# Splitting the attention stage's first operands ahead of it, and laying five key blocks as three and two

## The reference, cut to what matters

```
s = einsum('...qgrd,...kgd->...qgrk', q, k) * SCALE
mask = (dpos >= 0) & (dpos < WINDOW)          # window branch; selected branch: dpos >= 0
p = softmax(where(mask, s, NEG))
o = gates[0] * o_cmp + gates[1] * o_sel + gates[2] * o_win
x = x + rmsnorm(concat(ret_y, o) @ w_o); ...  # then the MLP
```

## Time and profile before

| What | us |
|---|---|
| Median of 3 runs | 1829.54 (1827.85 to 1830.1) |
| The profiled execution's own time | 1826.82 |
| Its span, first to last instruction | 1825.2 |
| TensorE busy | 1713.0 (94%) |
| VectorE busy | 838.9 (46%) |
| ScalarE busy | 618.1 (34%) |
| Mean granted clock of TensorE | 0.978 |

### The profile page before, as it was taken

How to read it: one execution, slowest core, us unless ns; L and a number is a source line. 1 busy time by engine, 2 the same in 40 slices (tenths; PEclk the granted TensorE clock), 3 DMA queues, 4 the chain that set the end, 5 groups by cost and what they waited for, 6 DMA issues and landing times. The chain is left out here.

```text
span 1825.2 us, 29596 instructions
## 1 busy us (share of the span) xinstructions
PE 1713.0 (94%) x11664; PEld 1511.1 (83%) x11664; DVE 838.9 (46%) x1606; ACT 618.1 (34%) x1188; POOL 148.9 (8%) x261
## 2 busy tenths in 40 slices
PE   5999999995999779999989999999999999999997
PEld 4989988994864655555549889999999999999997
DVE  5556342131116366677775675322332233223476
ACT  5222322210010156666655554202320232023343
POOL 1000000013534300000000110000000000000011
PEclk9999999997999799999999999999999999999999
DMA  8111011144966500000017533211111111111365
GB/s 292 47 48 48 24 48 42 47 104 116 239 180 190 153 17 1 1 1 1 1 45 198 174 119 93 66 47 47 47 47 47 47 47 47 47 47 47 110 177 166
DMA packets 215500, 148.98 MB, mean 82 GB/s; under 512 B 13565, under 2 KB 204882, under 8 KB 214978
## 3 DMA queue, kind: packets, MB, share of 16 engines
q1 hardware_dynamic: 180050, 99.38, 19.4%
q0 software_dynamic: 12848, 37.47, 6.7%
q10 hardware_dynamic: 22464, 10.23, 2.2%
HBM read 134.76 MB, written 16.47 MB: 83 GB/s over the span
## 5 line engine op out<-in xcount | busy, mean ns | idle before, releaser
L2077 PE MATMUL psum<-act_hi,whi 128*128 128x344 f32 x960 | 310.2, 323 | 8.6 <-DVE wlo L2196 5.6
L2077 PE MATMUL psum<-act_lo,whi 128*128 128x344 f32 x960 | 307.4, 320 | 0.0
L2077 PE MATMUL psum<-act_hi,wlo 128*128 128x344 f32 x960 | 307.4, 320 | 0.0
L2196 DVE TENSOR_TENSOR wlo<-wraw,whi 128x1024 fp32r<-128x1024 f32 x111 | 136.0, 1225 | 253.7 <-ACT whi L2093 253.5
L2077 PE MATMUL psum<-hidden_hi,whi 128*128 128x344 f32 x768 | 246.4, 321 | 0.0
L2077 PE MATMUL psum<-hidden_hi,wlo 128*128 128x344 f32 x768 | 245.3, 319 | 0.0
L2077 PE MATMUL psum<-hidden_lo,whi 128*128 128x344 f32 x768 | 245.2, 319 | 0.0
L2093 ACT ACTIVATE whi<-wraw 128x1024 fp32r<-128x1024 f32 x111 | 117.4, 1057 | 338.1 <-PE psum L2077 332.0
L231 PE MATMUL psum<-act_hi,whi 128*128 128x344 f32 x648 | 214.8, 331 | 4.1 <-DVE act_lo L404 4.1
L231 PE MATMUL psum<-act_hi,wlo 128*128 128x344 f32 x648 | 208.1, 321 | 0.0
L231 PE MATMUL psum<-act_lo,whi 128*128 128x344 f32 x648 | 208.1, 321 | 0.0
(11 more groups left out here) (366 smaller groups left out, 2474.7 us busy)
## 6 DMA issues: line engine op xcount, KB each, us to landing
wraw<-in_w_down SPq DMA_DIRECT2D x48, 512.0 KB, 3.7
wraw<-in_w_up SPq DMA_DIRECT2D x40, 512.0 KB, 4.1
wraw<-in_w_in SPq DMA_DIRECT2D x27, 512.0 KB, 3.8
wraw<-in_w_o SPq DMA_DIRECT2D x23, 512.0 KB, 4.6
h_features<-mixed_then_h POOLq DMA_DIRECT2D x24, 172.0 KB, 2.5
h_again<-h_features POOLq DMA_DIRECT2D x24, 172.0 KB, 3.0
x_rows<-in_x_prompt SPq DMA_DIRECT2D x4, 1024.0 KB, 9.2
dec_pages<-in_cache_sel_k SPq DMA_DIRECT2D x64, 64.0 KB, 3.0
```

The costliest lines, as they stand in the source:

```text
L2077: last = pe.matmul(ps[:, u % 3, 0:TN], wt[:, kt, :], xt[:, kt, cols], start=(kt == 0 and i == 0), stop=(kt == KT - 1 and i == 2))
L2196: dve.tensor_tensor(m.wlo[p % 2][:], wraw[raw_slot[p]][:], m.whi[p % 2][:].bitcast(F32), ALU.subtract).then_inc(lo_ready, 1)
```

## The change

Four things are changed.

1. The bf16 cast of the compressed bias and the split of query block 7 move from the start of the attention stage into the cache stage: ScalarE's part stands after its last copy of turned probabilities and ahead of its issues of value pages, VectorE's cast ahead of the fold matrix, and VectorE's part of the split after the second request. TensorE no longer waits for them at the start of the attention stage.
2. The first tile of `w_o` is split in the attention stage, by ScalarE at step 20 and by VectorE at step 21, into buffers of its own (`w_o_first_hi`, and `w_o_first_lo` over the raw tile). The raw tile lies elsewhere. The tail no longer splits it.
3. The first piece of attention outputs that the tail splits is cut in two, each with one row of tiles, and TensorE's unit 0 starts after the first of them.
4. Where five key blocks meet a query block they lie as three (384 columns, in the last three quarters of a bank) and two (256 columns, in the first half of the next). For the window the two are the oldest and the newest, read as one strided operand, and both masks are added by one bf16 matmul of 256 columns; the values are taken in the same order. The selected branch does it for query block 4, the window branch for blocks 4 to 7.

```diff
+            def three_and_two(bank, g, order, hi, lo, q):
+                a, b, c = order[0], order[3], order[4]
+                for n, k in enumerate((hi, lo)):
+                    pe.matmul(ps[:, bank, P:4 * P], q, k[:, g, a * P:(a + 3) * P], start=(n == 0), stop=(n == 1))
+                for n, k in enumerate((hi, lo)):
+                    pe.matmul(ps[:, bank + 1, 0:2 * P].rearrange("p (a n) -> p a n", n=P), q,
+                              k[:, g, 0:SEQ].rearrange("p (a n) -> p a n", n=P)[:, b:c + 1:c - b, :], start=(n == 0), stop=(n == 1))
...
-                if g == 0 and r == 0:
-                    pe.wait_ge(q_lo, 2 * ORDER.index(i) + 2)
+                if g == 0 and r == 0 and k:
+                    pe.wait_ge(q_lo, 2 * ORDER.index(i))
...
-                for a in range(lo, hi, 4):
-                    last = keys(2 + (a - lo) // 4, g, a * P, min(hi - a, 4) * P, win_hi, win_lo, q)
...
+                if i >= KW - 1:
+                    three_and_two(2, g, window_order(i), win_hi, win_lo, q)
+                    last = pe.matmul(ps[:, 3, 0:2 * P], m.ident_bf[:], m.edges_bf[:], start=False, stop=True, skip_group_check=True)
+                else:
+                    keys(2, g, 0, (i + 1) * P, win_hi, win_lo, q)
...
-            pe.wait_ge(casts, 1)
...
-            split_q(0)
             for k in range(len(steps) + 2):
...
+                if k == 20:
+                    act.wait_ge(first_loaded, 16)
+                    act.activation(m.first_hi[:], m.w_first[:], ACT.Copy).then_inc(first_hi, 1)
...
-            dve.tensor_copy(bias_bf[:], m.c("cmpbias").rearrange("p (a n) -> p a n", n=CP)).then_inc(casts, 1)
-            split_q(0)
...
+                if k == 21:
+                    dve.wait_ge(first_hi, 1)
+                    dve.tensor_tensor(m.first_lo[:], m.w_first[:], m.first_hi[:].bitcast(F32), ALU.subtract).then_inc(first_lo, 1)
...
+        def mix_parts(n):
+            a = n % 4
+            return (slice(0, 1), slice(1, 2)) if n == 0 else (slice(2 * a, 2 * a + 2),)
...
             split(0)
-            round_hi(0)
...
             split(0)
-            reduce_lo(0)
```

More of the change, by code:

```diff
@@ L1325, in _ @@
             act.activation(pnT[:], ps[0:DEC, 3, 0:2 * ROWS].rearrange("p (a b) -> p a b", b=ROWS), ACT.Copy).then_inc(p_copied, 1)
+            for e in range(2):
+                rows = slice(e * HD, (e + 1) * HD)
+                act.activation(m.q_split[(NB - 1) % 2][rows, :, e, :], m.nqT[rows, :, (NB - 1) * P:SEQ], ACT.Copy).then_inc(next_hi, 1)
             for b in range(4, DEC):
@@ L1477, in _ @@
             for b in range(DEC):
+                if b == 2:
+                    for e in range(2):
+                        rows, far = slice(e * HD, (e + 1) * HD), slice((1 - e) * HD, (2 - e) * HD)
+                        dve.wait_ge(next_hi, e + 1)
+                        dve.tensor_tensor(m.q_split[(NB - 1) % 2][far, :, e, :], m.nqT[rows, :, (NB - 1) * P:SEQ],
+                                          m.q_split[(NB - 1) % 2][rows, :, e, :].bitcast(F32), ALU.subtract).then_inc(next_lo, 1)
                 dve.wait_ge(v_used, b + 1)
@@ L1511, in stage_attend @@
         blk = [m.place(f"att_block_columns{i}", [P, 4, R], F32, m.ring + 22528 + 64 * i) for i in range(2)]
-        bias_bf = m.place("att_cmp_bias", [P, NB, CP], BF16, m.ring + 21888)
-        q_split = [m.place(f"att_q_split{i}", [P, NH // 2, 2, P], F32R, m.A + 57344 + 4096 * i) for i in range(2)]
+        q_split, bias_bf = m.q_split, m.bias_bf
         half = m.place("att_out_half", [HD, 4, P], F32, m.A + 65536)
@@ L1523, in window, with window_order, spare, scores @@
             return max(0, i - KW + 1), i + 1
+        def window_order(i):
+            lo, hi = window(i)
+            return [lo + 1, lo + 2, lo + 3, lo, lo + 4] if i >= KW - 1 else list(range(lo, hi))
+        def spare(blocks):
+            return P if blocks == 5 else 0
+        def scores(bank, blocks):
+            at = spare(blocks)
+            return ps[:, bank:bank + 2, :].rearrange("p a n -> p (a n)")[:, at:at + blocks * P]
         groups, first_group = [], []
@@ L1684, in _ @@
                     w = (i + 1) * P
-                    act.activation(p[k % 3][:, 0:w], ps[:, 0:2, :].rearrange("p a n -> p (a n)")[:, 0:w], ACT.Exp,
+                    act.activation(p[k % 3][:, 0:w], scores(0, i + 1), ACT.Exp,
                                    bias=c[:, 1:2], accum_out=c[:, 4:5]).then_inc(exps, 1)
```

86 lines of the change are left out of this document (45 added, 41 removed).

## The result

The changed kernel takes **1818.63 us** (median of 6 runs, 1817.23 to 1820.89) against 1829.24 us for the kernel before in the same comparison. The ratio is 0.9946 [0.9935, 0.9957], which is 9.9 us less (8 to 12; the two medians lie 10.6 us apart). The forecast was 7.0 us less, 1822.5 us, with a range of 1818.5 to 1826.

A forecast was written before the change was run, and what follows sets the result against it. TensorE, busy 94% of the span, was taken as the bound. 4.9 + 0.64 + 2.7 - 0.63 + 0.05 - 0.65 = 7.0 us off the median 1829.5 gave 1822.5 us, range 1818.5 to 1826.

The forecast's parts named there:

- The layout: Attention steps: window scores save 0.18 us in 29 steps, 4.9 us net; block 4's selected scores save 0.64 us.
- The deduction for ScalarE: Window scores: 0.3 us taken off the 5.2 us gain for steps where ScalarE's slack is under 0.2 us.
- The start: Attention stage's start: TensorE begins 2.17 us earlier, 3.05 if the clock stays up; 2.7 us taken.
- The cache stage: Casts and splits moved into the cache stage are covered by idle time: cost 0, at most 1.4 us.
- The first weight tile: Attention steps 20 to 22: splitting the tile there loses 0.53 and 0.1 us, together 0.63 us.
- The start of the tail: Tail: TensorE starts 1.97 us earlier, but this becomes a wait before unit 2; gain 0.05 us.
- The clock in the wait before unit 2: Tail: the new wait of 1 to 3 us can lower TensorE's clock; 0.65 us lost.
- the tail gains too: Rival, tail: second tile lands earlier or the wait costs no clock; gain 10, 1819.5 us; chance 0.15.
- Only the columns: Rival, window scores: 3.1 us in place of 4.9, and a cold start; gain 4.7, 1824.8 us; chance 0.17.
- ScalarE takes over: Rival, attention steps: ScalarE's copies and exponentials become the bound; about 1.5 us remain, 1828 us; chance 0.06.
- the slow operand: Rival, window scores: separated blocks read slower; gain 0.2 us at half pace, 1843 us at quarter pace; chance 0.04.

The follow-up runs named there:

- mask_last: Kernel before, with only the bf16 mask of the window's lower edge moved behind the last fp32r piece, no column saved: 1825.2 us, ratio 0.9974.
- all_three: Changed kernel with rows of x held until unit 2's tile landed, block 6 split at step 7, first weight tile's hi part at step 19: 1813.57 us, ratio 0.991.
- tail_alone: Kernel before with only the first weight tile split in the attention stage and shorter first pieces in the tail: 1828.27 us, ratio 1.0001.
- rows_later: Changed kernel, with GpSimd waiting in the tail for the second streamed weight tile before issuing the first rows of x: 1815.91 us, ratio 0.9933.
- layout_alone: Changed kernel with everything undone but the three-and-two key block layout: 1822.17 us, ratio 0.9968 to the kernel before.

## Why the prediction was right, and where it was off

**The layout (4.9 + 0.64 forecast).** Right, in size and in cause. Alone it gives 5.8 us (3.7 to 7.9), and its trace 6.03 us over steps 4 to 31, where the terms make 5.54. The price of a step is 0.89 us by the trace, 0.90 forecast. Both halves of the working were needed: mask_last shows the part that is no columns. Mask_last is worth 4.8 us by its ratio, though, and 3.4 by the means, where its trace has 1.9. The Trainium skill's rule that weight loads are pulled ahead ("TensorE: Matmul & The Clock Gate", section "Part 2: What happens when you issue a matmul"), by which the mask between the pieces would have cost only its columns, holds from one fp32r piece to the next (0.22 us ahead) and not across the bf16 mask (0.04 ahead), and the matmul takes 0.20 us there against 0.12. The deduction for ScalarE was a little too large. Steps 25 and 29, which I had given nothing from the selected block, became 0.19 and 0.20 us shorter while TensorE's wait in them grew from 0.34 to 0.46: they kept the window's share and lost the selected block's, as worked out.

**The start (2.7 forecast).** Right in mechanism, and the term that was mis-sized. It measured 5.1 us, twice (2.9 to 7.3), 4.6 and 4.7 by the means. I had 2.17 us for the pause and 0.5 for a clock that stays up half of the time. The table gives 3.0 for the rest and 1.6 for the clock, against 2.17 and 0.5. By the traces, the way from the barrier to the end of step 4 is 2.9 us shorter with the early split (27.7 us in the mean of the five that split block 6 in step 2, against 30.6 in the five without), and this has the clock of that way in it already; what the times have beyond it no trace shows. The working priced the clock only up to the second step; without the early split the low stretches go on to about 15 us after the barrier in three of five traces, and the first 20 us have 4.5 us more of low clock in the mean.

**The cache stage (0).** Right: VectorE still waits for TensorE before the copy that follows its part of the split (0.92 us), and the copies keep their distance of 2.65 us. The attention barrier, which varies too much to show a microsecond, lies no later with the early split (641.4 to 646.3, mean 643.8) than without it (643.2 to 646.1, mean 644.5).

**The first weight tile (-0.63).** Right: step 20 lost 0.52 us against its neighbours and 0.57 against all_three, where the split stands in step 19; it is ended by exactly the copy named. Steps 21 and 22 lost nothing.

**The start of the tail (+0.05).** Right, and the one that could most easily have gone wrong: a start 2.0 us earlier is worth nothing alone (0.2 us more by tail_alone, between 2.0 less and 2.4 more), because unit 2 waits for its tile. With the tile brought forward the 2 us appear (rows_later). The rule of the Trainium skill that transfers of all queues share 16 DMA engines ("Trainium Kernel Development and Optimization", section "Key Constraints") agrees with this: holding back 1.4 MB from POOL brought a tile of 0.5 MB from SP 3.6 us forward.

**The clock in the wait before unit 2 (-0.65).** Wrong: in none of the four traces with that wait does the clock fall in it or behind it. The low stretch at the tail's start is that of unit 0, from 942.0 to 945.4 us; before, TensorE worked in it from 954 to some 958.5. A fall that no term had took 1.3 us in steps 2 and 3 of the profiled execution.

**The sum.** 7.0 forecast, 9.9 measured (8 to 12), and 8.8 the second time, within the range by 0.13 us only. So that the time lies in the range is partly luck: the mechanisms were right but for the clock before unit 2, and the size of the start was not. Of the rivals, "the tail gains too" has the nearest time (1819.5) but the wrong cause, since the tail gained nothing. "Only the columns", "ScalarE takes over" and the slow operand are refuted by the step lengths.

**What stays open.** Mask_last gains 3.1 us by the means with the clock taken out and 1.9 by its trace; tail_alone loses 0.9 where its trace shows, beside low stretches of the clock (one of them late, which lengthens steps 32 to 63 by 1.5 us), nothing lost but 0.4 in step 20. The scatter of a mean is some 0.4 us for such a kernel even with the clock taken out, and the runs before come from three comparisons, so a microsecond may be chance; no run here tells. That a weight load starts late behind the bf16 mask is shown; whether the type does it, or something else in which the mask differs from a piece, is not, since no run had an fp32r matmul of 128 columns in its place. And why the clock falls in one execution of a kernel and not in the next was not tried.

## What to carry to other kernels

Before removing a wait, look for what else the next units need from the same barrier on, and count it from there: an engine that starts 2 us sooner gains nothing while a tile lands at a fixed time, and the cheap second edit, which holds back a transfer that nobody needs yet, is what cashes it in. Work that is moved into a busy stage goes into the step whose engine has idle time in front of its first instruction; one step aside it cost over 0.5 us. Count small matmuls by their start-to-start times in their real neighbourhood and not by their columns: 40% of the layout's gain was the order of the types. The start of a matmul's weight load, against the start of the matmul, shows where this happens.

## What the runs showed of the hardware

- A fp32r matmul of 256 columns took 0.20 us from start to start behind a bf16 one and 0.12 behind another fp32r one; a bf16 mask behind the last piece didn't lose this again (1.00 against 1.08 us). Its weight load started 0.04 us ahead of it behind the bf16 one, and 0.22 behind the fp32r one.
- A moving operand of two blocks of 128 columns 512 keys apart ran at the pace of adjoining columns (0.11 and 0.13 us for 256).
- 0.001 of mean granted clock went with 0.83 us of time, from one execution to the next (155 executions of twelve kernels).
- The granted clock was 0.53 over the first 13.8 us of the attention stage behind a pause of TensorE of 4.3 us (layout_alone), and 1.00 over its first 14.1 us behind a pause of 2.1 us (all_three). It fell early in five of five traces behind the longer pause and in two of eight behind the shorter.
- A tile of 512 KB issued second of several landed early enough for its copy to start 10.1 to 11.5 us after the barrier while 1.4 MB from POOL were under way, and 6.7 to 6.9 us after it without them, when it waited for TensorE and no longer for the tile.
